# Second layer's attention: the sink as first score column, one masked minimum that begins at the negated sink

## The chip, the cores and the metric

The kernel runs on one core of one Trainium2 chip. The metric is the device time of one execution in microseconds (us). The engines are TensorE (PE in the profile, with PEld for its weight loads), VectorE (DVE), ScalarE (ACT), GpSimd (POOL) and SyncE (SP). Each works through its own list of instructions in order, and they meet through semaphores.

## The reference, cut to what matters

The program computes a two-layer transformer block for 512 tokens of width 1024, followed by a second block of another kind. The change touches only the attention of the first block's second layer: 16 query heads, two key/value heads, a window of 128 keys, and one learned logit per head, the sink, that takes part in the softmax without having a value vector:

```
q, k, v = split(h @ w_in);  q = rope(q);  k = rope(k)
o = banded_attention(q, k, v, window=128, sinks)

# banded_attention, for each block of 128 queries
s = where(mask, q @ k.T * scale, -inf)
m = maximum(max(s), sink)
e = exp(s - m)
p = e / (sum(e) + exp(sink - m))
o = p @ v
```

## The kernel before, in words

The three other attentions of the program (`nsa` in the first layer, `na` and `ca` in the second block) run through the same code as this one, which is called `swa`; only a plan (`plan_swa`) differs. A plan lists groups of four units. In `swa` a group is one head (`sink=h`) and a unit `i` is one block `b` of 128 queries of that head: 16 heads x 4 blocks = 64 units. Block 0 sees 128 keys, blocks 1, 2 and 3 see 256 each.

There is no loop over units on the chip. Every engine has its own unrolled list, and each list is skewed against the others, so that several units are in flight. In iteration `i`:

- PE computes the scores of unit `i` (L785, two matmuls, into one of three PSUM banks), transposes the finished weights of unit `i-5` (L799, one 128x128 transpose per 128 keys), and every fourth time, in the iteration of block 3, multiplies a whole head's transposed weights by the values (L816, ten matmuls).
- DVE adds mask and scores with the sign turned, and takes the minimum of the row (L1591, one custom instruction and one that reads its accumulator into `stat_neg`), so that the minimum is the negated maximum. With a sink it then copies the negated sink into the column after the scores (L1597) and takes the smaller of the minimum and the negated sink into `stat_negs` (L1598). `link` puts a wait between the minimum and these two: the instruction raises the semaphore `dchain`, and DVE waits for it. Then come the reciprocal of the sum of unit `i-1` (L1603) and the low half of the transposed weights of unit `i-7` (L1613). In the iteration of block 1 the next head's queries are split (L1580); in block 3's, or the one before, the two halves of a finished head are added (L1621). In the lists these stand where the timeline shows them: L1621 and L1580 between block 2's L1613 and block 3's L1591.
- ACT takes the exponential of the scores and sums it (L1125), over 129 or 257 columns with the sink's; then it copies the high half of the transposed weights of unit `i-6` (L1137). The next head's queries are split in block 1's iteration (L1112), and the lower half of a finished head is copied in block 2's (L1153).
- POOL multiplies the exponentials by the reciprocal of their sum (L598). Its result is first read by PE four iterations later.

The waits that matter: ACT's exponential waits for DVE's `masked`; DVE's reciprocal waits for ACT's `exped` of the unit before; DVE's L1613 waits for ACT's L1137; and PE's transposes of unit `j` wait for DVE's L1613 of unit `j-3`, which DVE issued in the iteration before. SP's and ACT's DMA queues have next to nothing to do in this stage.

The scores tile `sc` has two buffers (`u % 2`), the weights tile `pr` eight.

Of the kernel before, what the change touches and what calls it, by code (L numbers as in the profile page):

```python
# [22 lines left out]
ALU = mybir.AluOpType  # L23
AX = mybir.AxisListType

P = 128
# [74 lines left out]
def build(nc, T, out):  # L101
# [463 lines left out]
    def _(pool):  # L565
# [22 lines left out]
        def scale_weights(which, fills):  # L588

            plan = PLANS[which]  # L590
            for i in range(4 * len(plan.groups)):
# [3 lines left out]
                pool.wait_ge(sem("inverted"), u + 1)  # L595
                w = plan.weights[i % len(plan.weights)][:, 0:nk]
                if grp["gate"] is None:
# [15 lines left out]
    def _(pe):  # L613
# [155 lines left out]
        def attention(which):  # L769
            plan = PLANS[which]  # L770
            n, u0, g0, s0 = 4 * len(plan.groups), c["unit"], c["groups"], c["splits"]
            for i in range(n + plan.av - 3):
# [16 lines left out]
                if plan.turn <= i < n + plan.turn:  # L789

                    j = i - plan.turn
                    grp, b, u = plan.groups[j // 4], j % 4, u0 + j
                    pe.wait_ge(sem("scaled"), u + 1)
                    banks = plan.turn_banks
                    if j >= len(banks):
                        pe.wait_ge(sem("pt_lo"), u - len(banks) + 1)
                    for a in range(0, grp["keys"][b], P):
                        m = min(P, grp["keys"][b] - a)
                        mm = pe.transpose(banks[j % len(banks)][0:m, a:a + P], plan.weights[j % len(plan.weights)][:, a:a + m], ident)  # L799
                    mm.then_inc(sem("pt_turned"), 1)  # L800
# [234 lines left out]
    def _(act):  # L1035
# [66 lines left out]
        def attention(which, before=None):  # L1102
            plan = PLANS[which]
            n, u0, g0 = 4 * len(plan.groups), c["unit"], c["groups"]
            for i in range(n + plan.out - 3):
# [8 lines left out]
                if i < n:  # L1114
# [6 lines left out]
                    if i >= ring:  # L1121
                        act.wait_ge(sem("pt_turned"), u - ring + 1)
                    neg = stat[0 if sink is None else 1][:, v:v + 1]
                    nk += sink is not None
# [309 lines left out]
    def _(dve):  # L1434
# [135 lines left out]
        def attention(which, before=None):  # L1570
# [3 lines left out]
            for i in range(n + plan.out - 2):  # L1574
# [7 lines left out]
                if i < n:  # L1582
# [5 lines left out]
                    if u >= 2:  # L1588
                        dve.wait_ge(sem("exped"), u - 1)

                    low = dve.tensor_tensor_reduce(sc[u % 2][:, 0:nk], plan.score_banks[i % len(plan.score_banks)][:, 0:nk], mask, -1.0, 3e38, ALU.add, ALU.min,  # L1591
                                                   stat[0][:, v:v + 1])
                    if grp["sink"] is None:
                        low.then_inc(sem("masked"), 1)
                    else:
                        link(low)
                        dve.tensor_copy(sc[u % 2][:, nk:nk + 1], sinks[:, 1, grp["sink"]:grp["sink"] + 1])  # L1597
                        dve.tensor_scalar(stat[1][:, v:v + 1], stat[0][:, v:v + 1], sinks[:, 1, grp["sink"]:grp["sink"] + 1], None, ALU.min)\  # L1598
                            .then_inc(sem("masked"), 1)
                if 1 <= i < n + 1:  # L1600
# [456 lines left out]
```

## Time and profile before

| what | us |
|---|---|
| median of 3 runs | 3001.21 |
| lowest, highest | 2999.03, 3004.59 |
| profiled execution | 3004.8 |
| its span, first to last instruction | 3003.0 |
| TensorE busy in the span | 2722.0 (91%) |
| VectorE busy | 1428.6 (48%) |
| `swa` attention, first L1591 to the first matmul of the layer after it | 1155.75 to 1267.33 |

The span is what the trace covers, and all times of the trace count from its start. The profiled execution took 1.8 us more than its span. A timeline row gives the start, the duration (of the last of several merged instructions its end is start plus duration), the engine, the line and operation, the output and inputs, and in brackets how long the engine stood idle before it and whom it waited for. The granted clock of TensorE has two levels, shown as 0.50 (1.2 GHz) and 1.00 (2.4 GHz); a mean between them means that the stretch had both.

### The profile page before, as it was taken

What the parts mean: (1) busy time and instruction counts of PE and PEld (TensorE: products, weight loads), DVE (VectorE), ACT (ScalarE), POOL (GpSimd) and SP (SyncE); (2) the same over time, 40 slices, a digit from 0 to 9 for tenths busy, and PEclk for the clock granted to TensorE, in tenths of its full rate; (3) what the DMA queues carried; (4) which work ended last, traced back from release to release, by engine and by line L of the source; (5) the groups of instructions that cost most, each with busy time, mean ns of one, the idle gap of its engine ahead of it and who ended that gap; (6) DMA issues with size and microseconds to landing.
All of it is one profiled execution on the core that took longest, in us unless ns stands there. A gap on an engine that the chain in (4) does not pass through costs nothing. (4 is left out here: it accounts for less than half of the span.)

```text
span 3003.0 us, 38041 instructions
## 1 busy us (share of the span) xinstructions
PE 2722.0 (91%) x12112; PEld 2184.4 (73%) x12112; DVE 1428.6 (48%) x2984; ACT 769.3 (26%) x1711; POOL 1766.6 (59%) x1019
## 2 busy tenths in 40 slices
PE   5799778889999987889999989999799989899998
PEld 4687555668888765767888767777587776687876
DVE  5657667543334258742121346666213834353462
ACT  2200666521111124621110132222102623200001
POOL 2636333337777635447777644444377966587784
PEclk9899788879999977579999889999799999899999
DMA  5455000015465320123333221211142322333232
GB/s 203 140 170 172 1 1 1 8 56 171 149 203 170 87 46 29 36 67 91 94 95 98 78 77 57 64 57 57 35 105 81 67 79 64 105 92 104 85 99 76
DMA packets 420407, 260.17 MB, mean 87 GB/s; under 512 B 62828, under 2 KB 411369, under 8 KB 413745
## 3 DMA queue, kind: packets, MB, share of 16 engines
q1 hardware_dynamic: 390368, 193.18, 22.3%
q10 hardware_dynamic: 29905, 65.31, 6.4%
q8 instruction: 71, 1.16, 0.2%
q14 instruction: 63, 0.52, 0.1%
HBM read 254.25 MB, written 8.10 MB: 87 GB/s over the span
## 5 line engine op out<-in xcount | busy, mean ns | idle before, releaser
L573 POOL TENSOR_TENSOR W<-RAW,zeros 128x1024 fp32r<-128x1024 f32 (+2 forms) x355 | 680.0, 1916 | 908.0 <-PE PA L641 697.2
L580 POOL TENSOR_TENSOR W<-RAW,W 128x1024 fp32r<-128x1024 f32 (+2 forms) x355 | 851.9, 2400 | 38.1 <-PE PA L645 11.9
L640 PE MATMUL PA<-H,W 128*128 128x512 f32 x1408 | 579.4, 412 | 40.8 <-DVE H L1525 29.6
L641 PE MATMUL PA<-H,W 128*128 128x512 f32 x1408 | 561.9, 399 | 0.0
L640 PE MATMUL PA<-A,W 128*128 128x512 f32 x944 | 382.8, 405 | 16.2 <-DVE A L1635 11.4
L641 PE MATMUL PA<-A,W 128*128 128x512 f32 x944 | 380.9, 404 | 0.0
L640 PEld LDWEIGHTS PA<-H,W 128*128 128x128 f32 x1408 | 270.8, 192 | 139.7 <-issue 40.8
L645 PE MATMUL PA<-H,W 128*128 128x512 f32 x1408 | 355.7, 396 | 0.0
L641 PEld LDWEIGHTS PA<-H,W 128*128 128x128 f32 x1408 | 272.7, 194 | 57.7 <-issue 4.6
L645 PEld LDWEIGHTS PA<-H,W 128*128 128x128 f32 x1408 | 270.5, 192 | 57.4
L645 PE MATMUL PA<-A,W 128*128 128x512 f32 x944 | 243.4, 400 | 0.0
L640 PEld LDWEIGHTS PA<-A,W 128*128 128x128 f32 x944 | 182.4, 193 | 64.4 <-issue 14.6
L641 PEld LDWEIGHTS PA<-A,W 128*128 128x128 f32 x944 | 182.1, 193 | 43.9
L645 PEld LDWEIGHTS PA<-A,W 128*128 128x128 f32 x944 | 179.5, 190 | 44.2
L600 POOL TENSOR_SCALAR pr<-pr,stat_inv,gate 128x128 f32<-128x128 f32 (+1 forms) x192 | 106.3, 555 | 177.6 <-DVE stat_inv L1603 175.9
L598 POOL TENSOR_SCALAR pr<-pr,stat_inv 128x256 f32<-128x256 f32 (+2 forms) x112 | 130.0, 1164 | 85.7 <-DVE stat_inv L1603 84.0
L1701 DVE SCALAR_TENSOR_TENSOR PA<-PA,tmp 128x512 f32<-128x512 f32 x64 | 44.8, 700 | 247.4 <-ACT tmp L1188 247.4
L799 PE MATMUL PT<-cst,pr 128*128 128x128 f32 (+1 forms) x507 | 113.4, 325 | 50.6 <-DVE H L1613 42.9
L1125 ACT ACTIVATE pr<-sc,stat_neg 128x128 f32<-128x128 f32 (+3 forms) x240 | 123.1, 513 | 127.8 <-DVE stat_neg L1591 122.8
L1188 ACT ACTIVATE tmp<-PA 128x512 f32<-128x512 f32 x64 | 38.3, 598 | 385.9 <-PE PA L645 385.9
L799 PEld LDWEIGHTS PT<-cst,pr 128*128 128x128 f32 (+1 forms) x507 | 66.6, 159 | 84.6 <-POOL pr L600 49.2
L675 PE MATMUL PA<-H,W 128*128 128x512 f32 x280 | 116.7, 417 | 0.0
(325 smaller groups left out, 4143.5 us busy)
## 6 DMA issues: line engine op xcount, KB each, us to landing
AD<-in_ada_w_dram ACTq DMA_DIRECT2D x40, 1024.0 KB, 5.5
RAW<-in_w_in_dram SPq DMA_DIRECT2D x160, 256.0 KB, 3.1
RAW<-in_mlp_w_up_dram SPq DMA_DIRECT2D x128, 256.0 KB, 3.1
RAW<-in_mlp_w_down_dram SPq DMA_DIRECT2D x128, 256.0 KB, 3.0
RAW<-in_w_up_dram SPq DMA_DIRECT2D x88, 256.0 KB, 3.1
RAW<-in_nsa_w_in_dram SPq DMA_DIRECT2D x40, 256.0 KB, 3.9
RAW<-in_w_down_dram SPq DMA_DIRECT2D x16, 384.0 KB, 3.4
RAW<-in_swa_w_in_dram SPq DMA_DIRECT2D x20, 256.0 KB, 3.5
```

The lines of the kernel that those rows point to most:

```text
L573: e.tensor_tensor(W[0][:, s, 0:kc], RAW[:, s, 0:kc], zeros[:, 0:1].rearrange("p (a b) -> p a b", b=1).broadcast_to([P, kc, P]), ALU.add).t ...
L580: e.tensor_tensor(W[1][:, s, 0:kc], RAW[:, s, 0:kc], W[0][:, s, 0:kc].bitcast(F32), ALU.subtract).then_inc(w_split, 1)
L598: pool.tensor_scalar(w, w, inverse, None, ALU.mult).then_inc(sem("scaled"), 1)
L600: pool.tensor_scalar(w, w, inverse, grp["gate"][b], ALU.mult, ALU.mult).then_inc(sem("scaled"), 1)
L640: pe.matmul(PA[s][:, 0:n], W[0][:, s, k], hi, start=(k == 0), stop=False)
L641: mm = pe.matmul(PA[s][:, 0:n], W[0][:, s, k], lo, start=False, stop=False)
L645: mm = pe.matmul(PA[s][:, 0:n], W[1][:, s, k], x[0][:, k, 0:n], start=False, stop=(k == kc - 1))
L675: pe.matmul(PA[s][:, :], W[0][:, s, k], H[0][:, k, :], start=(k == 0), stop=False)
L799: mm = pe.transpose(banks[j % len(banks)][0:m, a:a + P], plan.weights[j % len(plan.weights)][:, a:a + m], ident)
L1125: act.activation(plan.weights[i % ring][:, 0:nk], sc[u % 2][:, 0:nk], ACT.Exp, bias=neg, scale=-1.0, accum_out=stat[2][:, v:v + 1]).then_i ...
L1188: act.activation(tmp[q][:], PA[s][:], ACT.Relu).then_inc(sem("mlp_relu"), 1)
L1701: dve.scalar_tensor_tensor(PA[s][:], PA[s][:], 0.0, tmp[q][:], ALU.max, ALU.mult).then_inc(sem("mlp_square"), 1)
```

## The change

Where a group has a sink, the sink's column is now the first of `sc` and `pr` (column 0), the scores and weights follow from column 1. The negated sink is copied into column 0 of `sc` only in the iterations of blocks 0 and 1, once for each of the two buffers of `sc`, and blocks 2 and 3 find it there. The masked minimum takes the negated sink as the value it begins from, as a per-partition operand, instead of the number 3e38. The separate minimum, its tile `stat_negs` and the `link` are gone. POOL scales from column 1, PE transposes from column 1, and ACT reads its bias from `stat_neg` and works on the same 129 or 257 columns as before. The other attentions issue what they issued before.

```
-                w = plan.weights[i % len(plan.weights)][:, 0:nk]
+                at = int(grp["sink"] is not None)
+                w = plan.weights[i % len(plan.weights)][:, at:at + nk]
...
-                        mm = pe.transpose(banks[j % len(banks)][0:m, a:a + P], plan.weights[j % len(plan.weights)][:, a:a + m], ident)
+                        mm = pe.transpose(banks[j % len(banks)][0:m, a:a + P], plan.weights[j % len(plan.weights)][:, at + a:at + a + m], ident)
...
-                    neg = stat[0 if sink is None else 1][:, v:v + 1]
+                    neg = stat[0][:, v:v + 1]
...
-                    low = dve.tensor_tensor_reduce(sc[u % 2][:, 0:nk], plan.score_banks[i % len(plan.score_banks)][:, 0:nk], mask, -1.0, 3e38, ALU.add, ALU.min,
-                                                   stat[0][:, v:v + 1])
-                    if grp["sink"] is None:
-                        low.then_inc(sem("masked"), 1)
-                    else:
-                        link(low)
-                        dve.tensor_copy(sc[u % 2][:, nk:nk + 1], sinks[:, 1, grp["sink"]:grp["sink"] + 1])
-                        dve.tensor_scalar(stat[1][:, v:v + 1], stat[0][:, v:v + 1], sinks[:, 1, grp["sink"]:grp["sink"] + 1], None, ALU.min)\
-                            .then_inc(sem("masked"), 1)
+                    at, least = 0, 3e38
+                    if grp["sink"] is not None:
+                        at, least = 1, sinks[:, 1, grp["sink"]:grp["sink"] + 1]
+                        if b < 2:
+                            dve.tensor_copy(sc[u % 2][:, 0:1], least)
+                    dve.tensor_tensor_reduce(sc[u % 2][:, at:at + nk], plan.score_banks[i % len(plan.score_banks)][:, 0:nk], mask, -1.0, least,
+                                             ALU.add, ALU.min, stat[0][:, v:v + 1]).then_inc(sem("masked"), 1)
```

On DVE, in the iterations of blocks 0 and 1 of one head, the order before is this (ISA is the masked minimum and the read of its accumulator; PS and PA are PSUM banks with scores, `cst` holds the masks, `H` the transposed weights):

```order
L1591 ISA sc,stat_neg<-PS,cst 128x128
L1591 ISA stat_neg 128x1
L1597 COPY sc<-sinks 128x1
L1598 TENSOR_SCALAR stat_negs<-stat_neg,sinks 128x1
L1603 RECIPROCAL stat_inv<-stat_sum 128x1
L1613 TENSOR_TENSOR H<-PA,H 128x2x128
L1591 ISA sc,stat_neg<-PS,cst 128x256
L1591 ISA stat_neg 128x1
```

And on DVE at the same place of the program now:

```order
L1597 COPY sc<-sinks 128x1
L1598 ISA sc,stat_neg<-PS,cst,sinks 128x128
L1598 ISA stat_neg 128x1
L1603 RECIPROCAL stat_inv<-stat_sum 128x1
L1613 TENSOR_TENSOR H<-PA,H 128x2x128
L1597 COPY sc<-sinks 128x1
```

The copy has moved ahead of the masked minimum (behind the two waits, for the scores and for the exponential that used the buffer before), the separate minimum is gone, and the reciprocal stands directly behind the read of the accumulator. On DVE in block 3's iteration of a head the order before is:

```order
L1580 TENSOR_TENSOR QS<-Y,QS 64x512
L1591 ISA sc,stat_neg<-PA,cst 128x256
L1591 ISA stat_neg 128x1
L1597 COPY sc<-sinks 128x1
L1598 TENSOR_SCALAR stat_negs<-stat_neg,sinks 128x1
L1603 RECIPROCAL stat_inv<-stat_sum 128x1
L1613 TENSOR_TENSOR H<-PT,H 128x128
```

and now, on DVE, in block 3's iteration:

```order
L1582 TENSOR_TENSOR QS<-Y,QS 64x512
L1598 ISA sc,stat_neg<-PA,cst,sinks 128x256
L1598 ISA stat_neg 128x1
L1603 RECIPROCAL stat_inv<-stat_sum 128x1
L1613 TENSOR_TENSOR H<-PT,H 128x128
```

Both small instructions are gone there. The lists of PE, ACT and POOL hold the same instructions in the same order as before.

## Rows read from the trace of the kernel before

**Rows 1.** Busy us (instructions) of PE, PEld, DVE, ACT, POOL; granted clock, DMA, by stretch
```profile
1156.00:1173.20 17.20, 11.19 (x48) 9.55 (x47) 14.27 (x72) 11.31 (x37) 10.17 (x11) 0.50 0.01 1
1173.20:1203.38 30.18, 22.89 (x126) 19.33 (x125) 26.73 (x130) 21.01 (x68) 16.15 (x20) 0.78 0.00 1
1203.38:1250.37 46.99, 41.89 (x177) 36.33 (x178) 38.66 (x182) 31.98 (x101) 24.08 (x29) 0.50 0.00 1
...
1169.20:1174.20 5.00, 4.83 (x22) 4.32 (x21) 3.35 (x18) 2.17 (x9) 2.11 (x4) 0.52 0.01 3
```

**Rows 2.** Groups of DVE in the attention: the two small instructions
```profile
L1598 DVE TENSOR_SCALAR stat_negs<-stat_neg,sinks 128x1 f32<-128x1 f32 x64 | 13.0, 204 | 0.0
...
L1597 DVE COPY sc<-sinks 128x1 f32<-128x1 f32 x64 | 9.8, 154 | 2.2
```

**Rows 3.** Timeline, a head at the low clock: a unit with its sink instructions
```profile
1210.09 0.29 DVE L1591 CUSTOM_DVE_ANT_0 sc<-PS,cst 128x128 f32<-128x128 f32 x1 [0.67 <-PE PS L785]
1210.43 0.15 DVE L1597 COPY sc<-sinks 128x1 f32<-128x1 f32 x1
1210.50 0.20 DVE L1598 TENSOR_SCALAR stat_negs<-stat_neg,sinks 128x1 f32<-128x1 f32 x1
1210.62 0.15 DVE L1603 RECIPROCAL stat_inv<-stat_sum 128x1 f32<-128x1 f32 x1
1210.69 0.41 DVE L1613 TENSOR_TENSOR H<-PA,H 128x256 fp32r<-128x256 f32 x1
1210.74 0.40 ACT L1125 ACTIVATE pr<-sc,stat_negs 128x129 f32<-128x129 f32 x1 [0.66 <-DVE stat_negs L1598]
```

**Rows 4.** Timeline, first layer's attention: a unit of the same size without sink
```profile
408.15 0.29 DVE L1591 CUSTOM_DVE_ANT_0 sc<-PS,cst 128x128 f32<-128x128 f32 x1 [2.09 <-PE PS L785]
408.37 0.16 DVE L1603 RECIPROCAL stat_inv<-stat_sum 128x1 f32<-128x1 f32 x1
408.49 0.40 ACT L1125 ACTIVATE pr<-sc,stat_neg 128x128 f32<-128x128 f32 x1 [1.97 <-DVE stat_neg L1591]
```

**Rows 5.** Three DVE lines elsewhere: immediate operand; pointer, column 1; pointer, column 0
```profile
L1701 DVE SCALAR_TENSOR_TENSOR PA<-PA,tmp x64: 699/700/700, 680.1 to 1662.8; 128x512 f32<-128x512 f32 x64
L1999 DVE SCALAR_TENSOR_TENSOR tmp<-PA,cols,tmp x44: 749/750/752, 2622.4 to 2922.0; 128x511 f32<-128x511 f32 x44
L2000 DVE SCALAR_TENSOR_TENSOR tmp<-PA,cols,tmp x44: 749/749/751, 2623.2 to 2922.8; 128x511 f32<-128x511 f32 x44
```

**Rows 6.** Timeline, the same low-clock head: where ACT and PE set the pace
```profile
1211.24 0.45 PE L799 MATMUL PA<-cst,pr 128*128 128x128 f32 x1 [0.31 <-DVE H L1613]
1212.69 0.36 ACT L1137 ACTIVATE H<-PT 128x256 fp32r<-128x256 f32 x1
1213.08 0.42 DVE L1613 TENSOR_TENSOR H<-PT,H 128x256 fp32r<-128x256 f32 x1
1213.65 0.66 PE L799 MATMUL PT<-cst,pr 128*128 128x128 f32 x2 [0.28 <-DVE H L1613]
1216.81 0.29 DVE L1591 CUSTOM_DVE_ANT_0 sc<-PS,cst 128x128 f32<-128x128 f32 x1 [0.67 <-PE PS L785]
```

**Rows 7.** Timeline, a head at the full clock: minima of two blocks 0 and block 3, exponentials
```profile
1191.61 0.29 DVE L1591 CUSTOM_DVE_ANT_0 sc<-PS,cst 128x128 f32<-128x128 f32 x1 [0.39 <-PE PS L785]
1196.26 0.42 DVE L1591 CUSTOM_DVE_ANT_0 sc<-PS,cst 128x256 f32<-128x256 f32 x1
1197.03 0.51 ACT L1125 ACTIVATE pr<-sc,stat_negs 128x257 f32<-128x257 f32 x1 [1.33 <-DVE stat_negs L1598]
1197.17 0.28 DVE L1591 CUSTOM_DVE_ANT_0 sc<-PS,cst 128x128 f32<-128x128 f32 x1
1197.81 0.40 ACT L1125 ACTIVATE pr<-sc,stat_negs 128x129 f32<-128x129 f32 x1
```

**Rows 8.** Timeline, PE: the last gap ahead of the second rise of the clock
```profile
1187.64 0.66 PE L799 MATMUL PA<-cst,pr 128*128 128x128 f32 x2 [0.16 <-DVE H L1613]
```

**Rows 9.** Busy time, columns as in rows 1: the two microseconds of the second rise
```profile
1190.00:1192.00 2.00, 2.00 (x13) 1.84 (x13) 1.51 (x10) 0.87 (x3) 0.88 (x1) 0.74 0.02 4
```

More of the change, by code:

```diff
@@ L796, in attention @@
                         pe.wait_ge(sem("pt_lo"), u - len(banks) + 1)
+                    at = int(grp["sink"] is not None)
                     for a in range(0, grp["keys"][b], P):
                         m = min(P, grp["keys"][b] - a)
-                        mm = pe.transpose(banks[j % len(banks)][0:m, a:a + P], plan.weights[j % len(plan.weights)][:, a:a + m], ident)
+                        mm = pe.transpose(banks[j % len(banks)][0:m, a:a + P], plan.weights[j % len(plan.weights)][:, at + a:at + a + m], ident)
                     mm.then_inc(sem("pt_turned"), 1)
```

## The prediction, made before the changed kernel ran

> **What bounds the kernel now.** I read the view of busy time by stretch first [rows 1], then the timeline of single heads [rows 3, 6, 7], and last the same code without a sink in the first layer [rows 4]. The attention of the second layer takes 1155.75 to some 1266 us, 110 of 3003. No engine is busy all the time in it. From 1203.38 to 1250.37 PE is busy 41.89 of 46.99 us, DVE 38.66, ACT 31.98 [rows 1]: seven heads of 6.71 us each, all at the low clock (0.50), and each a repetition of the one in [rows 3, 6]. Between 1173.20 and 1203.38 stand five heads at a mean clock of 0.78; a head that lies wholly at the full clock takes 1197.17 - 1191.61 = 5.56 us [rows 7]. Before 1173.20 stand three heads in which also keys and values are split, and DVE is busy 14.27 of 17.20 us [rows 1].
>
> What ends last is a circle through three engines. At the low clock it goes, from one block 0 to the next [rows 3, 6]: DVE starts the masked minimum (1210.09); ACT can start its exponential 0.65 later (1210.74), waiting only for DVE; from there ACT works back to back through five instructions, two exponentials, two copies of transposed weights and the split of the next queries, to the end of L1137 (1212.69 + 0.36 = 1213.05); DVE's L1613 starts at 1213.08, and PE, which has stood idle for 0.28 us, starts the transposes of block 3's iteration at 1213.65; behind them it runs without a gap through a head's values and the next scores, and DVE, idle for 0.67, starts the next block 0 at 1216.81. So 0.65 + 2.34 + 0.57 + 3.16 = 6.72. The reader should see that of the four units of a head only block 0's sink instructions lie on this circle. Those of blocks 1 and 2 run while ACT catches up, those of block 3 while PE multiplies the values.
>
> **The change, part by part.** *One unit.* With a sink the minimum starts at 1210.09, the reciprocal at 1210.62 and the exponential at 1210.74: 0.53 and 0.65 us later [rows 3]. Without, the same size gives 408.15, 408.37 and 408.49: 0.22 and 0.34 [rows 4]. So copy, second minimum and the wait of the `link` cost 0.31 us on either path. Busy time would say 0.154 + 0.204 = 0.36 [rows 2], but the two overlap by their starts (0.07 apart); I take 0.31.
>
> The Trainium skill, page "VectorE: DVE Perf Modes", section "The DRAIN you can't avoid", says of a semaphore behind each of a chain of copies that it "costs nothing extra here". By that the `link` would be free. The rows do not agree: the small copy starts 0.34 after the minimum, where the reciprocal of a unit without sink starts at 0.22, so the wait is 0.12 of the 0.31. By the page a unit would gain 0.19.
>
> *The operand.* The minimum now begins from a per-partition value. The trace has no such form. The nearest rows: an instruction with an immediate takes 700 ns for 512 columns, one with a per-partition operand 750 for 511 [rows 5]. So 0 to 0.06 us a unit; I take 0.05. Net, a unit gives 0.26.
>
> *The copy that stays.* In blocks 0 and 1 it stands behind the wait for the scores and ahead of the minimum, so in block 0 it is on the circle. It costs between 0.07 (the distance of the two small instructions, 1210.43 to 1210.50 [rows 3]) and its own 0.15 [rows 2]; I take 0.07, since the minimum reads nothing of it, as L1598 does not.
>
> *The odd column.* `sc` is written and `pr` read from column 1. For DVE the rows show nothing: 750 with output and input at column 1, 749 with the output at column 0 [rows 5]. For PE and POOL no row has it; I take nothing, and the bound is a rival below. The Trainium skill, page "Vector Engine (DVE) Microarchitecture Reference", section "Measured stream behaviour on trn2", speaks against the change here: pairs that start on an odd word stream at 1.30 ns a column instead of 1.05. It measured pairs that hop; as an estimate for 256 columns it would be 0.06 us a unit and take a fifth of the gain. Rows 5 do not show it for a contiguous run.
>
> *A head at the low clock.* The circle loses 0.31, gains 0.05 and 0.07: 0.19 us. Everything else may shrink more, but the circle then is what is late: ACT's five instructions are unchanged. Bounds: 0.31 (both free) and 0.10 (0.06 and 0.15). There are 46.99 / 6.71 = 7 such heads, and of the five before them, which took 30.18, (5 x 6.71 - 30.18) / (6.71 - 5.56) = 2.9 are worth a full-clock head and 2.1 a low-clock one. 9.1 x 0.19 = 1.7, and the last head, up to its values, another 0.2.
>
> *A head at the full clock.* Here PE is idle often, and two routes from block 3 to the next block 0 end together: DVE's (minimum 1196.26, next minimum 1197.17, its exponential 1197.81) and ACT's (exponential 1197.03, a copy, exponential 1197.81) [rows 7]. DVE's route loses 2 x 0.26 - 0.07 = 0.45, ACT's only the 0.26 ahead of block 3's exponential, because the 0.78 from one exponential to the next is ACT's own work. So 0.26, and 2.9 x 0.26 = 0.8.
>
> *The first three heads.* DVE works through them almost without a gap, and for five units (head 0's block 3 to head 1's block 3) nothing else is late: 5 x 0.26 - 2 x 0.07 = 1.2. Head 0's first exponential and the following head's block 0 add 0.19 each before PE is the bound: 1.5 in all (1.1 to 2.2).
>
> *Elsewhere.* Behind the last minimum nothing changes; the end moves with it. The other attentions issue the same. POOL's scaling is first read four iterations later, so what it gains or loses by an earlier start is covered.
>
> The sum at the clock as it is granted now: 1.5 + 0.8 + 1.7 + 0.2 = 4.2 us, with bounds 2.9 and 6.2. The profiled execution took 3004.8 for a span of 3003.0, the median is 3001.21; I take the sum from the median: 2997.0.
>
> **The rivals.**
>
> *A: the sum alone, 2997.0.* For it speaks that the seven low-clock heads are copies of one another, and the clock may stay as it is. Against it, what follows.
>
> *B: the shorter gaps bring the full clock back, and this is my forecast.* The rows show where the clock rose: around 1174.0, after PE had run for 5 us nearly without a gap (4.83 busy of the 5.00 us from 1169.20, at a mean clock of 0.52 [rows 1]), and at 1191.0 (a mean of 0.74 over 1190 to 1192 is 1.0 us at 1.00 [rows 9]), after one gap of 0.16 at 1187.64 [rows 8] and PE busy all through 1190 to 1192. In each of the seven low-clock heads PE has three gaps, 0.28 and 0.31 [rows 6] and one near the 0.16 of [rows 8]; the stretch between the first two is 4.0 us long (from 1213.65 to 1211.24 + 6.71 - 0.31 = 1217.64 [rows 6]). Now block 0's L1613 comes earlier by 0.31 - 0.05 - 0.07 = 0.19, so the gap of 0.31 that ends this stretch falls to some 0.13, and the next one stays near it. The unbroken work becomes some 5 us long, as before the first rise, with one gap like that before the second. The Trainium skill, page "TensorE: Matmul & The Clock Gate", section "The HAM clock gate", says that "the default state is throttled, and activity releases the throttle". The rows agree so far; that seven heads with this activity stayed low shows that it does not follow each time. Price: a full-clock head now is 5.56 - 0.26 = 5.30, a low-clock one 6.71 - 0.19 = 6.52, so each head that changes over gives 1.22. The two stretches at the full clock are together (0.78 - 0.50) / 0.50 x 30.18 = 16.9 us [rows 1], 3 heads of 5.56, so 1.5 heads each. One to two more of them among the seven are 1.5 to 3 heads, 1.8 to 3.7 us; I take the middle, 2.8. 4.2 + 2.8 = 7.0: **2994.2**, with a range of its own of 2990.5 to 2996.
>
> *C: the clock goes the other way.* A faster DVE shifts the work, and the two stretches at the full clock are lost: 2.9 heads x 1.22 = 3.5 of the 4.2. 3000.5.
>
> *D: reading from an odd column slows PE's transposes; this is the slower side.* A low-clock head has seven transposes of about 0.33 us (0.66 for two [rows 6]). PE has 6.71 - 41.89 / 7 = 0.73 us to spare in such a head, less 0.19 after the change, so up to 0.54 / 7 = 0.08 a transpose costs nothing; past that it is on the circle. If each took a second 0.33, a head would take 5.98 + 2.3 = 8.3 instead of 6.71, and nine such heads 14 us more: 3015 less the gain elsewhere, about 3013. Nothing in the rows shows it, and the operands of the transposes are plain 4-byte columns.
>
> *E: nothing is gained,* because the minimum with a pointer operand costs a separate step of the size of what was removed (0.31). Then 3001. [Rows 5] speak against it.
>
> **How the numbers follow.** B 0.46, A 0.34, C 0.08, D 0.07, E 0.05. About 0.2% (6 us, so below 2995.2) is what a measurement of this kernel can tell from no change. B lies below it nine times in ten, A once in eight: faster 0.45; D is the slower 0.07; the rest, 0.48, is within. The range takes in B's far end and A with its bounds (2995.0 to 2998.3), and reaches towards C: 2990 to 3000.
>
> **What would show it.** After: 32 copies (0.15 us) instead of 64 and no 128x1 minimum; DVE's busy time in the stage lower by some 64 x 0.204 + 32 x 0.154 - 64 x 0.05 = 15 us, of which at most half shows in the span; from the minimum's start to the exponential's 0.39 us in block 0 instead of 0.65, and 0.05 more in the minimum's own duration; low-clock heads 6.5 us apart, full-clock heads 5.3; ACT's wait for the minimum still there in block 3 (now 1.33 [rows 7]). The step on the clock is wrong if heads from the ninth on are all at 0.50; the step on PE if a transpose pair at the low clock takes more than 0.66; the step on ACT if low-clock heads fall by more than 0.31. Later stages should stand as before; a difference there is not from this change's cost, though it may be from the clock.

## The result, and the profile after

The changed kernel took 2982.51 us (median of 5 runs, 2979.69 to 2985.99), the kernel before, beside it on the same chip, 2999.03 (5 runs, 2995.81 to 3004.59). The ratio is 0.9945, with a 95% interval of 0.993 to 0.996: 16.5 us faster, where 7 were forecast, and outside the range. In a later comparison on one chip, which is the better measure since it has more runs, the same kernel took 2988.52 against 2999.34, a ratio of 0.9966 (0.9953 to 0.9979): 10.8 us, and again below the range of 2990 to 3000.

The page of the changed kernel, span and busy time by engine:

```profile
span 2982.6 us, 37945 instructions
...
PE 2699.8 (91%) x12112; PEld 2163.9 (73%) x12112; DVE 1418.0 (48%) x2888; ACT 768.4 (26%) x1711; POOL 1766.7 (59%) x1019
```

Busy time in the four parts of the second layer's attention, from the first masked minimum to the first matmul of the layer after it (busy us and instructions of PE, PEld, DVE, ACT, POOL, then granted clock and DMA). The first three rows answer to those of [rows 1]:

```profile
1152.78:1168.12 15.34, 10.53 (x49) 8.99 (x49) 12.71 (x55) 11.24 (x37) 10.16 (x11) 0.54 0.01 2
1168.12:1195.06 26.94, 18.34 (x125) 14.63 (x123) 24.01 (x101) 20.51 (x68) 15.90 (x20) 1.00 0.00 1
1195.06:1238.38 43.32, 34.38 (x178) 29.14 (x178) 34.58 (x142) 31.73 (x101) 24.39 (x29) 0.73 0.00 1
1238.38:1251.43 13.05, 7.44 (x52) 5.95 (x51) 9.38 (x32) 9.06 (x25) 4.25 (x5) 0.89 0.00 1
```

The column to read is the clock, third from the end. Heads are counted from 0. Heads 3 to 7 stood at a mean of 0.78 before and are at 1.00 now; heads 8 to 14 stood at 0.50 and are at 0.73; the last head with its way to the end has 0.89. Part by part (before from the same views):

| part | before | after | gain | forecast |
|---|---|---|---|---|
| first three heads | 17.45 | 15.34 | 2.1 | 1.5 |
| next twelve heads | 77.17 | 70.26 | 6.9 | 0.8 + 1.7 + 2.8 = 5.3 |
| last head's block 0 to the end | 16.96 | 13.05 | 3.9 | 0.2 |
| the stage | 111.58 | 98.65 | 12.9 | 7.0 |

The spans differ by 20.4 us, so 7.5 lie outside the stage: it began 3.0 earlier, and what follows it took 4.5 less. That belongs to no step of the change: over the traces of one and the same kernel the stage began between 1147.30 and 1155.75 (before) and between 1150.66 and 1152.78 (after).

DVE's small instructions, groups of the changed kernel (busy us, mean ns, idle before), and ACT's wait for the minimum (us in total, times, longest). They answer to [rows 2]:

```profile
L1598 DVE CUSTOM_DVE_ANT_0 sc<-PS,cst,sinks 128x256 f32<-128x256 f32 x32 | 15.4, 480 | 0.4
...
L1597 DVE COPY sc<-sinks 128x1 f32<-128x1 f32 x32 | 4.8, 149 | 6.2 <-PE PS L786 5.0 <-PE PA L786 0.9
...
ACT pr L1127 <- DVE stat_neg L1598: 22.8, 24, 1.4
```

64 small minima and 32 copies are gone. The masked minimum over 256 columns takes 480 ns. ACT waited 31.8 us for it before, in 33 places, and waits 22.8 in 24 now.

A head at the low clock, timeline; it answers to [rows 3, 6]:

```profile
1225.27 0.15 DVE L1597 COPY sc<-sinks 128x1 f32<-128x1 f32 x1 [0.91 <-PE PS L786]
...
1225.34 0.34 DVE L1598 CUSTOM_DVE_ANT_0 sc<-PS,cst,sinks 128x128 f32<-128x128 f32 x1
...
1225.60 0.16 DVE L1603 RECIPROCAL stat_inv<-stat_sum 128x1 f32<-128x1 f32 x1
1225.68 0.40 DVE L1613 TENSOR_TENSOR H<-PT,H 128x256 fp32r<-128x256 f32 x1
...
1225.72 0.41 ACT L1127 ACTIVATE pr<-sc,stat_neg 128x129 f32<-128x129 f32 x1 [0.72 <-DVE stat_neg L1598]
...
1226.23 0.45 PE L801 MATMUL PT<-cst,pr 128*128 128x128 f32 x1
...
1228.64 0.66 PE L801 MATMUL PA<-cst,pr 128*128 128x128 f32 x2 [0.32 <-DVE H L1613]
...
1231.86 0.34 DVE L1598 CUSTOM_DVE_ANT_0 sc<-PA,cst,sinks 128x128 f32<-128x128 f32 x1
```

From the minimum to the exponential it is 1225.72 - 1225.34 = 0.38 us, where it was 0.65. The heads are 1231.86 - 1225.34 = 6.52 apart, as forecast. The three gaps of PE in such a head (0.28, 0.31, 0.17) have become one: the transposes of 1226.23 start with no gap ahead of them, those of 1228.64 with 0.32. From 1228.64 PE then has no gap before 1235.16, 6.2 us of unbroken work; the prediction had some 5 us. A pair of transposes still takes 0.66, so reading from column 1 costs PE nothing that shows.

A head at the full clock; it answers to [rows 7]:

```profile
1172.63 0.48 DVE L1598 CUSTOM_DVE_ANT_0 sc<-PS,cst,sinks 128x256 f32<-128x256 f32 x1
...
1173.15 0.51 ACT L1127 ACTIVATE pr<-sc,stat_neg 128x257 f32<-128x257 f32 x1 [1.20 <-DVE stat_neg L1598]
...
1173.36 0.34 DVE L1598 CUSTOM_DVE_ANT_0 sc<-PS,cst,sinks 128x128 f32<-128x128 f32 x1
...
1173.93 0.39 ACT L1127 ACTIVATE pr<-sc,stat_neg 128x129 f32<-128x129 f32 x1
```

From minimum to exponential in block 3 it is 0.52 instead of 0.77, and the 0.78 from one exponential to the next are unchanged: ACT's own work, as the prediction had it. It is 0.25 here, for the 0.26 of the sum.

Where the clock went up and down in the changed kernel, in stretches of one level each:

```profile
1167.00:1201.00 34.00, 23.31 (x160) 18.85 (x160) 29.22 (x122) 25.80 (x86) 20.34 (x25) 1.00 0.00 1
1201.00:1208.00 7.00, 6.55 (x29) 5.67 (x29) 5.40 (x24) 4.98 (x18) 4.00 (x6) 0.51 0.00 0
1208.00:1221.50 13.50, 8.88 (x58) 6.83 (x57) 11.47 (x49) 10.86 (x35) 8.19 (x10) 1.00 0.01 2
1221.50:1238.50 17.00, 15.22 (x67) 13.66 (x67) 12.69 (x49) 11.25 (x36) 8.60 (x10) 0.50 0.00 0
1238.50:1249.00 10.50, 7.32 (x52) 5.80 (x50) 7.74 (x28) 7.42 (x22) 4.25 (x5) 0.99 0.01 2
```

And the two stretches at the full clock in the kernel before, with all that follows them:

```profile
1174.00:1181.00 7.00, 4.35 (x29) 3.38 (x28) 6.48 (x33) 5.50 (x19) 4.36 (x6) 0.99 0.00 0
...
1191.00:1201.50 10.50, 6.67 (x48) 5.47 (x47) 9.29 (x48) 8.64 (x28) 6.72 (x8) 0.99 0.01 2
1201.50:1250.37 48.87, 43.77 (x186) 38.04 (x186) 40.30 (x189) 32.41 (x102) 24.35 (x29) 0.50 0.00 1
```

17.5 us at the full clock before, 34 + 13.5 + 10.5 = 58 after. The full clock came 18 us after the start of the stage before (at 1174) and 14 after it now (at 1167), and then it did not go away after 7 us but after 34.

PE at the end of the stage, after and then before, the three products with the values and the first matmul of the next layer:

```profile
1241.27 1.33 PE L818 MATMUL PO<-H,VV 128*128 128x256 f32 x10
...
1244.57 1.33 PE L818 MATMUL PO<-H,VV 128*128 128x256 f32 x10
...
1247.08 1.36 PE L818 MATMUL PO<-H,VV 128*128 128x256 f32 x10 [0.93 <-DVE H L1613]
1251.43 0.76 PE L641 MATMUL PA<-A,W 128*128 128x512 f32 x1 [3.00 <-DVE A L1635]
```

```profile
1254.02 2.38 PE L816 MATMUL PO<-H,VV 128*128 128x256 f32 x10
...
1258.19 2.38 PE L816 MATMUL PO<-H,VV 128*128 128x256 f32 x10
...
1261.94 2.40 PE L816 MATMUL PO<-H,VV 128*128 128x256 f32 x10 [0.93 <-DVE H L1613]
1267.33 0.76 PE L640 MATMUL PA<-A,W 128*128 128x512 f32 x1 [3.00 <-DVE A L1635]
```

Hardly anything of the change runs here (three minima, after the last head's block 0), and yet the part from the last head's block 0 on shrank by 3.9 us. The third stretch at the full clock lies exactly here: ten matmuls take 1.33 instead of 2.38, three times 1.05. This stretch is not the change's alone, though. In a second trace of the kernel before (before_again, below) the same part had a mean clock of 0.75 and took 13.76 us, in the third (before_third) 17.07 at the low clock:

```profile
1248.27:1262.03 13.76, 8.92 (x52) 7.25 (x52) 10.16 (x38) 9.08 (x25) 4.42 (x6) 0.75 0.01 1
```

### The profile page after: what moved, and what is told of

The parts are those of the page before. It is cut to its first block and busy times, and to the rows that moved or that the text cites. A ratio compares the mean times of both kernels' runs of the same rounds, so it can differ in the third digit from the quotient of the medians.

```text
span 2982.6 us, 37945 instructions
## 1 busy us (share of the span) xinstructions
PE 2699.8 (91%) x12112; PEld 2163.9 (73%) x12112; DVE 1418.0 (48%) x2888; ACT 768.4 (26%) x1711; POOL 1766.7 (59%) x1019
## 5 line engine op out<-in xcount | busy, mean ns | idle before, releaser
L1127 ACT ACTIVATE pr<-sc,stat_neg 128x31 f32<-128x31 f32 (+6 forms) x304 | 153.7, 506 | 152.2 <-DVE stat_neg L1598 146.8
```

The source lines that it names most:

```text
L1127: act.activation(plan.weights[i % ring][:, 0:nk], sc[u % 2][:, 0:nk], ACT.Exp, bias=neg, scale=-1.0, accum_out=stat[2][:, v:v + 1]).then_i ...
```

## The experiments

All are of this kernel on one core. "Stage" is from the first masked minimum to the first matmul of the next layer in the run's trace; ratios are to the kernel before on the same chip, as the record has them; they can differ by up to 0.0013 from the quotient of two medians.

| run | median us (range, runs) | ratio, 95% | stage |
|---|---|---|---|
| before_again | 2995.39 (one) | | 108.69 |
| before_third | 2998.42 (2992.59 to 3004.74, 12) | 1.000, 0.9989 to 1.0011 | 111.81 |
| after_again | 2981.75 (one) | | 98.51 |
| after_third | 2988.52 (2981.59 to 2997.30, 10) | 0.9966, 0.9953 to 0.9979 | 98.63 |
| before_pe | 2986.32 (2980.65 to 2990.14, 7) | 0.9956, 0.9941 to 0.9972 | 102.85 |
| after_pe | 2984.74 (2977.17 to 2986.55, 5) | 0.9938, 0.9917 to 0.9960 | 95.58 |
| after_pe_second | 2981.32 (2976.84 to 2984.61, 5) | 0.9941, 0.9923 to 0.9958 | 95.59 |
| after_pe_nsa | 2998.91 (2993.09 to 3003.11, 10) | 0.9997, 0.9986 to 1.0008 | 95.69 |
| column_only | 2997.80 (2992.10 to 3004.09, 10) | 0.9992, 0.9979 to 1.0005 | 108.24 |
| minimum_only | 2997.64 (2991.48 to 3001.68, 10) | 0.9992, 0.9980 to 1.0005 | 107.61 |
| minimum_only_pe | 2983.60 (2977.94 to 2989.78, 8) | 0.9951, 0.9937 to 0.9964 | 96.45 |
| back_block0 | 3002.14 (2996.07 to 3005.19, 10) | 1.0001, 0.9989 to 1.0014 | 111.55 |
| back_block0_pe | 2987.16 (2978.92 to 2987.79, 5) | 0.9952, 0.9935 to 0.9970 | 97.91 |
| back_blocks123 | 2997.47 (2994.43 to 3006.45, 10) | 0.9993, 0.9978 to 1.0007 | 111.00 |
| back_blocks123_pe | 2995.81 (2985.35 to 3000.69, 10) | 0.9987, 0.9974 to 1.0000 | 106.82 |

The first profile of before had a stage of 111.58, that of after 98.65.

**Is the clock's pattern a matter of one execution?** Both kernels again, unchanged.

> The kernel before, unchanged, profiled once more, to see what of the first trace repeats. If the clock in the second layer's attention is set by this code and its timing, the seven heads 6.71 us apart at a clock of 0.50 come back, and the stage (first masked minimum to the first matmul of the layer behind it) takes 111.6 us within 2. If the clock there is chance, the stage differs by 5 us or more from the first trace. The profiled execution of the first trace took 3004.8 us, the slowest of five; this one should lie nearer to 2999.

> The changed kernel, unchanged, profiled once more. First trace: low-clock heads 6.52 us apart, full-clock heads 5.3 to 5.7, clock 1.00 from about 1167 to 1201 and again twice later, stage 98.7 us. If the pattern is set by the code, the stage takes 98.7 within 2 us; if it is chance, it lies anywhere up to 108 us (all heads at the low clock: 16 x 6.52 less the shorter first heads, plus the tail).

From the fourth head on, the changed kernel's heads had the same lengths to 0.01 us in the traces of after, after_again and after_third, although the stage began at 1152.78, 1150.66 and 1152.48. Its 58 us at the full clock belong to the kernel. The kernel before is looser: it has some 17, 30 and 24 us of full clock in its three traces, which makes its stage 111.6, 108.7 and 111.8. Against before_again the stage gains 10.2 us, not 12.9. The forecast for before_again (111.6 within 2) missed by 0.9, that for after_again and after_third held.

**What is left of the change when the clock is taken out?** The first matmul of each unit's scores is issued twice; the second writes over the first's result, so nothing is left out or changed.

```
 # PE, ahead of the loop over the score terms (L785)
+                    if grp["sink"] is not None:
+                        pe.matmul(bank, terms[0][0], terms[0][1], start=True, stop=True)
```

> The kernel before, with the first matmul of every unit's scores issued twice (64 more matmuls of 128 or 256 columns, whose result the next one overwrites). Theory K (most of the gain was clock): the extra work fills PE's gaps, the clock rises earlier and stays longer, heads go from 6.71 towards 5.6 us, and the kernel with more work is faster than before by 4 to 11 us. Theory S (the gain was the shorter serial path, clock changes are chance): the clock stays as it is, each low-clock head grows by one matmul on the circle, 0.2 us, and the kernel is slower by 1 to 3 us.

> The changed kernel with the same extra matmul per unit. Theory K: the clock is now full in nearly all heads, so the changed kernel gains at most the 3 low-clock stretches it had left (about 4 heads x 1.1 = 4 us), and against the kernel before with the extra matmul only the serial part remains, 3 to 5 us. Theory S: the difference between the two kernels stays at 13 us or more in this stage, with and without the extra matmul.

Heads 3 to 7 and 8 to 14, first before_pe and then after_pe (columns as above):

```profile
1168.99:1197.61 28.62, 20.57 (x145) 16.95 (x143) 26.50 (x130) 20.69 (x68) 15.90 (x20) 1.00 0.00 1
1197.61:1240.12 42.51, 31.76 (x203) 26.65 (x203) 38.07 (x184) 30.95 (x99) 23.55 (x29) 0.92 0.00 1
```

```profile
1170.38:1197.31 26.93, 20.63 (x145) 16.94 (x143) 24.16 (x101) 20.52 (x68) 15.91 (x20) 1.00 0.00 1
1197.31:1237.13 39.82, 29.59 (x203) 24.17 (x203) 34.73 (x142) 30.73 (x99) 23.47 (x29) 1.00 0.00 1
```

64 matmuls that compute nothing new make the kernel before 13 us faster, 6 to 9 of them in the stage (102.85 against the three stages of before); the rest lies outside it and is not explained. after_pe stands at the full clock for the last 82 us of the stage without a break. Where both kernels have the full clock, the change gives (28.62 - 26.93) / 5 = 0.34 us in each of heads 3 to 7, 5.95 - 5.69 = 0.26 in each later head, and 0.5 from the last head's block 0 on (13.92 to 13.42). The first three heads give 17.80 - 15.41 = 2.4, but there the clock is mostly low in both. The whole stage goes from 102.85 to 95.58: 7.3, of which some 0.8 is two heads of before_pe (6.57 and 6.16) in which the clock fell for some 3 us each. The serial gain is thus some 6.5 us, above the sum's 4.2.

In the time of the whole kernel little of it can be seen here: the medians of before_pe and after_pe are 1.6 us apart (2986.32 and 2984.74), and their two spans are alike (2984.2 and 2984.3), since after_pe's stage begins 3.8 us later and what follows it takes 3.6 longer. Where these 7.4 us come from is open, so the terms below are those of the stage.

**Which half of the change does it?** First, the column alone:

```
+                    at = int(grp["sink"] is not None)         # scores from column 1
+                        if b < 2: dve.tensor_copy(sc[u % 2][:, 0:1], negated sink)
 # the minimum begins at 3e38; link and the separate minimum stay
```

> Half of the change: the sink's column is first and copied twice a head, but the masked minimum begins at 3e38 and the wait and the separate 128x1 minimum stay. From the start of a minimum to its exponential: 0.65 less the 0.07 of the copy that stood between, 0.58 us; in block 0 the copy now stands ahead and takes the 0.07 back. Serial theory: low-clock heads stay 6.71 us apart, full-clock heads lose 0.07; nothing measurable, 2997 to 3000, unless the clock pattern shifts. Rival (the copies are what cost): low-clock heads fall to 6.5 and the kernel takes over half of the gain.

Then the minimum alone:

```
-... mask, -1.0, 3e38, ALU.add, ALU.min, ...); link(low); dve.tensor_copy(...); dve.tensor_scalar(...)
+dve.tensor_copy(sc[u % 2][:, nk:nk + 1], least)               # every unit, column last
+... mask, -1.0, least, ALU.add, ALU.min, ...)
```

> The other half: the minimum begins at the negated sink, no wait, no separate minimum; the column stays last and is copied in every unit, ahead of the minimum. Serial theory: all of the gain on the circle, less 0.07 us in blocks 2 and 3: low-clock heads 6.52 apart, full-clock heads 5.7 to 5.8, stage 99 to 101 us, total 2983 to 2986. Rival (the odd column or the copies matter): it differs from the changed kernel by over 5 us.

Neither half alone gives anything that can be measured (2997.8 and 2997.6), and together they give 11 to 16 us. For column_only that was expected; for minimum_only 2983 to 2986 was, and this forecast failed. It is no accident of one trace: in all ten executions of either the mean clock of the kernel was 0.907 to 0.916, where the changed kernel mostly has 0.919 to 0.924. The price of each instruction is nonetheless seen apart. The masked minimum in column_only (scores from column 1, begins at an immediate), as a group:

```profile
L1598 DVE CUSTOM_DVE_ANT_0 sc<-PS,cst 128x256 f32<-128x256 f32 x32 | 13.5, 421 | 0.4
```

and in minimum_only (scores from column 0, begins at the pointer operand):

```profile
L1594 DVE CUSTOM_DVE_ANT_0 sc<-PS,cst,sinks 128x256 f32<-128x256 f32 x32 | 15.2, 474 | 0.0
```

So writing from the odd column on costs DVE nothing by itself (421 ns, the mean of before too), and the operand costs 0.05 us. Heads 8 to 14 of column_only and of minimum_only:

```profile
1203.04:1250.03 46.99, 41.87 (x178) 36.29 (x178) 38.15 (x170) 31.88 (x101) 24.26 (x29) 0.50 0.00 1
```

```profile
1193.97:1239.34 45.37, 40.39 (x178) 35.08 (x176) 35.51 (x156) 31.53 (x98) 23.64 (x28) 0.54 0.00 1
```

column_only has the heads of the kernel before, 6.71. minimum_only has within 0.02 us the 6.52 of the changed kernel in its low-clock heads, but the clock stays at 0.54 where the changed kernel has 0.73, and from the last head's block 0 on it needs 16.51, not 13.05.

**Which unit of a head carries the gain?** In the changed kernel the wait of `link`, a copy and a second minimum are put back, in block 0 or in blocks 1 to 3. Their results are read by nobody, but ACT's exponential waits for the second minimum, as in the kernel before.

```
+                    back = grp["sink"] is not None and b == 0      # or: b > 0
+                    if back:
+                        link(low)
+                        dve.tensor_copy(sc[u % 2][:, nk + 1:nk + 2], least)
+                        dve.tensor_scalar(stat[1][:, v:v + 1], stat[0][:, v:v + 1], least, None, ALU.min).then_inc(sem("masked"), 1)
```

> The changed kernel with wait, copy and separate 128x1 minimum put back in block 0 of each head alone (the result is the same and unused): 16 x 0.31 us. Circle as I drew it: at the low clock block 0 is on it in full, heads 6.52 + 0.31 = 6.83 us; at the full clock the route through ACT has 0.18 us of slack there, so 5.69 + 0.13 = 5.8. Rival (DVE's busy time sets the pace and a unit is a unit): a third of what blocks 1 to 3 cost.

> The changed kernel with the same three things put back in blocks 1, 2 and 3 and not in block 0: 48 x 0.31 us. Circle: at the low clock blocks 1 and 2 have about 0.5 us of slack beside ACT, so 0.62 more costs 0.13, heads 6.65 us; at the full clock block 3's 0.31 is ahead of its exponential and on the route, 5.69 + 0.31 = 6.0. Rival (DVE's busy time): three times what block 0 costs at either clock, 0.9 a head if that costs 0.31.

Heads 8 to 14 of back_block0:

```profile
1204.04:1251.87 47.83, 41.56 (x178) 36.06 (x176) 36.08 (x155) 31.50 (x98) 23.48 (x28) 0.50 0.00 1
```

47.83 / 7 = 6.83: the 0.31 come back whole (6.52 to 6.83) from one block in four, as the circle of the prediction says. With the other three put back, a head wholly at the low clock still takes 6.52, not the 6.65 that I expected: the slack of blocks 1 to 3 is larger than I took it. But both kernels lose all of the 11 to 16 us (3002.1 and 2997.5, with mean clocks of 0.905 to 0.915 in all their executions). In time, three of four units free of the extra work are worth nothing, nor is the fourth alone.

**Is it the clock that these four lose by?** The doubled matmul in three of them; column_only was not run with it.

> The half with the new minimum and a copy in every unit, plus the extra matmul per unit that kept the clock up in the two kernels before. Clock theory: it was slow (2997.6) only because the clock stayed low from its 1190th us on; with the extra matmul the clock is full from the fourth head on, full-clock heads are within 0.1 us of the changed kernel's 5.69, the stage takes 96 to 97 us and the kernel 2983 to 2987. Rival (the copies in blocks 2 and 3 cost much by themselves): the stage stays over 100 us.

> Put back in block 0 alone, with the extra matmul. Full clock throughout, so the serial price of block 0 alone shows: full-clock heads 0.13 us longer than the changed kernel's 5.69, stage 95.6 + 2 = 97.6 us. If a unit is a unit, 0.31 a head, 100.5 us.

> Put back in blocks 1, 2 and 3, with the extra matmul. Full clock throughout: block 3's 0.31 us is ahead of its exponential and on the route, blocks 1 and 2 are beside ACT, so heads of about 6.0 us (0.31 more) and a stage of 100 to 102 us. If a unit is a unit, 0.9 a head, 110 us.

Heads 8 to 14 of minimum_only_pe, of back_block0_pe and of back_blocks123_pe:

```profile
1194.25:1234.50 40.25, 29.62 (x203) 24.15 (x203) 35.58 (x157) 30.72 (x99) 23.44 (x29) 1.00 0.00 1
```

```profile
1196.06:1236.89 40.83, 29.63 (x203) 24.22 (x203) 35.79 (x157) 31.55 (x99) 23.50 (x29) 1.00 0.00 1
```

```profile
1199.67:1241.64 41.97, 29.23 (x203) 24.17 (x203) 38.55 (x184) 30.72 (x99) 23.48 (x29) 1.00 0.01 1
```

Yes. minimum_only goes from 2997.6 to 2983.6 and back_block0 from 3002.1 to 2987.2 with the same 64 matmuls. Divided by seven, the heads take 5.75, 5.83 and 6.00, against 5.69 in after_pe: the copy in blocks 2 and 3 costs 0.06 a head, what is put back in block 0 0.14, what is put back in blocks 1 to 3 0.31. With the clock held the price of each part can be read from the heads, and each is what the prediction's route through the full-clock head says (0.13 and 0.31 were expected); left alone they can't be told from the time. back_blocks123_pe is the exception in time (2995.8): heads 3 to 7 and the end were not all at the full clock, its end took 17.16, and its stage 106.82 where 100 to 102 was expected. So for this one the runs do not show that the clock alone is what it loses by.

**Does the first layer's attention want it too?** The doubled matmul also there, 256 instead of 64.

```
+                    if which in ("swa", "nsa"):
+                        pe.matmul(bank, terms[0][0], terms[0][1], start=True, stop=True)
```

> The changed kernel with the first scores matmul of every unit issued twice in the first layer's attention as well (mean clock there 0.81 between 400 and 600 us). If the clock is what that stage lacks too, it rises to 1.0 and the stage (281 us from its first minimum to the layer behind it) loses 5 to 15 us, which would beat both kernels. If PE's own work is the bound there, the extra 192 matmuls add up to 192 x 0.2 = 38 us at the full clock less what fits in the gaps: slower by 5 to 30 us.

The same window of 280 us, first after_pe, then after_pe_nsa. The masked minima of that attention run from 308.2 to 576.5 in the one and from 304.6 to 591.0 in the other:

```profile
300.00:580.00 280.00, 220.03 (x1059) 165.70 (x1059) 189.71 (x823) 188.09 (x630) 106.29 (x192) 0.83 0.00 1
```

```profile
300.00:580.00 280.00, 242.20 (x1228) 192.57 (x1229) 179.19 (x778) 179.77 (x596) 100.95 (x181) 0.82 0.00 1
```

No. PE is busy 22 us more in the window, the clock does not rise (0.83 and 0.82), and the second layer's attention starts at 1168.47 instead of 1154.97. The 192 matmuls cost some 13 us here, with nothing back from the clock.

**How large is the gain when it is measured again?** Both kernels and the best version once more, on one chip.

> The kernel before against itself, on the chip of the next two. Ratio 1.000 within 0.001. Its trace gives a third sample of the stage (111.6 and 108.7 us so far) and of the last 400 us of the program (401.8 and 399.1 so far): if the latter has two modes that the change does not choose, it is 399.1 or 401.9 again.

> The changed kernel, third trace. Stage 98.6 within 0.5 if the clock's pattern in it is set by its timing; the median some 16 us below before. Outside the stage the changed kernel gained about 4 us in the medians: if that is chance of single traces, the parts outside agree with the kernel before within their own scatter (2.7 us in the last part, 1.3 in the first panel behind the stage, 3 ahead of it).

> The changed kernel with the extra matmul per unit, beside the changed kernel on the same chip. Its stage was 95.6 us against 98.6, so by the stage alone it should be 3 us faster than the changed kernel; its first median was 2 us slower. If the 3 us hold, the medians are 2979 to 2981; if something outside gives them back, 2982 to 2985.

The order holds: 2998.4 (before), 2988.5 (after), 2981.3 (after with the doubled matmul, the best version, 7.2 us below the changed kernel beside it; their ranges still overlap by 3 us). Of these 7.2 the stage shows 3.0 (98.63 to 95.59), and in the first two comparisons the two versions could not be told apart (0.9945 and 0.9938), so how much the doubled matmul adds to the change is not settled. Each execution also lists its mean granted clock. Of the changed kernel's sixteen, twelve have 0.919 or more and a median of 2985.2, and four, all in this comparison, have 0.912 to 0.914 and a median of 2990.5. The kernel before has 0.907 to 0.916, the version with the doubled matmul 0.923 to 0.928. So the full clock that the change wins is not won in each execution, and that may be part of why 16.5 became 10.8. No trace shows one of those four, so where they lose it is open.

## Why the prediction was wrong, step by step

The step that failed is the clock's term, and with it the range. It stood at 2.8 us, for one or two more stretches at the full clock among seven heads, and at nothing behind the last minimum. In the first pair of traces the clock gave some 3.4 us in the twelve heads and 3.4 more from the last head's block 0 on. The serial term, 4.2, was short by some 2 us beside it.

**Right: the circle and its terms.** A low-clock head went from 6.71 to 6.52, block 0 put back gives 6.83, blocks 1 to 3 put back leave the low-clock heads as they are, and a later full-clock head went from 5.95 to 5.69 with the clock held. The `link` is most likely part of the price: what is put back in block 0 costs 0.31, and without a cost of the wait 0.19 would be left; no run takes the wait out alone. The Trainium skill ("VectorE: DVE Perf Modes", section "The DRAIN you can't avoid") has a semaphore in a chain of copies cost nothing; this case's 0.31 does not agree with that for a minimum and the instructions behind it. The pointer operand was taken at 0.05 and measures 0.05 alone, 0.06 together with the odd column (474 and 480 ns). column_only and minimum_only say that it is the operand's, but for 6 ns. The estimate from the odd-word figure of the Trainium skill ("Vector Engine (DVE) Microarchitecture Reference", section "Measured stream behaviour on trn2"), 0.06 us, has the same size by coincidence: a contiguous run written from an odd column does not show it here (421 ns either way).

**Right in kind: case B, its size in part by luck.** Two gaps of PE went, further than worked out (0.31 to none for a forecast of 0.13; 0.17 to none, where it was to stay), and there is more full clock. In the twelve heads 6.9 us were gained for 5.3 forecast. Of these some 3.5 are serial by the prices at the full clock (5 x 0.34 + 7 x 0.26) and 3.4 the clock's, for which 2.8 stood in the sum.

**Mis-sized: what a head gives that changes over.** The sum took 1.22 us (6.52 - 5.30). Its full-clock head (5.56, less 0.26) came from heads 3 to 7 alone, and four of those do take 5.24 to 5.42 now. Among the later heads, for which the price was meant, a full-clock head takes 5.69 in the changed kernel and 5.95 in before_pe, so a change-over gives 6.52 - 5.69 = 0.83. The seven heads had 6 + 13.5 = 19.5 us of full clock, 3.4 heads for the 1.5 to 3 forecast. More heads at a smaller price (3.4 x 0.83) make 2.8, the very term of the sum; that it fits is luck.

**Mis-sized: the serial sum, by about a third.** The first three heads gave 2.1, and 2.4 with the doubled matmul, for 1.5 with an upper bound of 2.2; full-clock heads 3 to 7 gave 0.34 for 0.26. In both the sum let another engine be the last as soon as DVE is not; which engine it was in fact was not traced. Of DVE's own time the forecast said 15 us less: the groups give some 14 (13.0 + 9.8 - 4.8 - 3.6), the busy time of the stage only 9.5 (90.1 to 80.7), most likely since it counts overlapping instructions once.

**Failed: "Behind the last minimum nothing changes; the end moves with it."** It was right of the instructions and wrong of the time. The part from the last head's block 0 on gave 3.9 us, 0.5 of it serial and the rest PE's matmuls at the full clock. It is the largest single miss (0.2 forecast), and it needed no new mechanism: the last head stands at the same low clock as the seven before it, and the forecast let the new stretches fall among those seven only. The size of the miss hangs on the trace, too: the changed kernel took 13.05 to 13.15 in all three of its traces, the kernel before 16.96, 13.76 and 17.07.

**Failed: the number of stretches.** The text looked at where the clock rose and asked whether PE's unbroken work gets long enough. But the gain came mostly from the clock not falling: the first stretch lasts 34 us instead of 7. And unbroken work, the sign that B went by, did not always bring it back: the changed kernel ran from 1221.5 to 1238.5 with PE busy 15.22 of 17.0 us at the low clock, the 6.2 us without a gap from 1228.64 in the midst of it. At the full clock PE was busy 4.35 of the 7.0 us and 6.67 of the 10.5 before, 23.31 of the 34 and 8.88 of the 13.5 after, and 29.59 of the 39.82 of after_pe's seven heads, in which the clock did not fall. That gives no rule: before_pe kept the full clock for its last 33.5 us (from 1220.19) with PE busy 22.33, about as densely as in the changed kernel's stretch of 13.5. The Trainium skill says that "activity releases the throttle" ("TensorE: Matmul & The Clock Gate", section "The HAM clock gate"). before_pe and the four others with the doubled matmul in this stage agree with it, after_pe_nsa in the first layer does not show it; how much it takes here, the runs do not tell.

**Failed: the range.** Its faster end was B with two more full-clock stretches among the heads. No case let the clock win over the whole stage, though the price of that was in the rows: 7 heads of 6.52 - 5.30 = 1.2. A case "full clock to the end", 4.2 of serial gain, 7 x 1.22 = 8.5 for the heads and 3 x 1.05 = 3.2 for the products with the values, gives 2985 and would have put both measured medians near or within the range. It would have come near by two errors that cancel in part: the heads' price is 0.83 (7 x 0.83 = 5.8), and the serial gain some 6.5.

**Open.** The medians differ by 16.5 us in one comparison and by 10.8 in the other, the stages by 10.0 to 13.3. What of the first lies outside the stage is scatter that both kernels show, and its cause was not looked for. Nor is it settled why the clock falls at 1201.0 and 1221.5 in the changed kernel and not in after_pe, and why the changed kernel keeps it for 34 us where minimum_only, back_block0 and back_blocks123 don't.

## What to carry to other kernels

Where an attention stage stands between the two clock levels, a serial saving is worth its own size only if the clock stays as it was; cost the stage once at either level, up to its last instruction, and let the range reach both. To see what an edit is really worth, hold the clock with matmuls whose result is overwritten and compare the stages at one level: here that turned results that seemed to contradict each other into prices of 0.06, 0.14 and 0.31 us a head. The same filler may be worth as much as the edit (13 us for 64 matmuls), or be a plain loss (14 us) in a stage whose clock does not answer, so measure it stage by stage. And take the price of a head from the heads it is meant for: in the changed kernel full-clock heads 3 to 6 take 5.24 to 5.42 us and the later ones 5.69.

## What the hardware showed that I had not expected

- More TensorE work made the kernel faster: 64 more matmuls of 128 or 256 columns, 2999.5 to 2986.3 us. On top of the change it was 2988.5 to 2981.3 in one comparison and nothing clear in the first.
- Gains did not add. The column alone 0.9992, the minimum alone 0.9992, both 0.9966 and 0.9945. minimum_only differs from the changed kernel by a 0.15 us copy in two of four units (and the sink's place), 0.06 us a head with the clock held, and stays 9 us above it (2997.6 and 2988.5, on two chips, each with a ratio of its own to the kernel before).
- A stage's clock pattern can be a fixed property of a kernel (the changed one, three traces with the same head times) or vary from run to run (the kernel before, 17 to 30 us at the full clock in three traces).
- A contiguous run of 4-byte columns from an odd column costs nothing that shows: DVE writes it in 421 ns for 256 columns as before (6 ns more with the pointer operand, 480 for 474), PE transposes it in 0.66 us a pair, and POOL's scaling takes 944 ns in the mean for 943.
